# Softmax weights transposed by VectorE and a round trip through HBM, in place of TensorE

## What is computed

```
def _memory_attention(q, mem, w_kv):            # every layer, 4 heads of 64
    ...
    probs = softmax(einsum('bshd,bmhd->bhsm', q, km))
    return einsum('bhsm,bmhd->bshd', probs, vm)
...
w = probs[:, 0] - lam * probs[:, 1]             # layers 0 and 3, 6 heads of 128
return einsum('bhqk,bkhe->bqhe', w, v)
```

## Time and profile before

| | |
|---|---|
| median of 3 runs | 1246.14 us (1246.03 to 1246.64) |
| profiled execution, its span | 1244.7 us |
| TensorE busy | 1235.2 us, 99% of the span |
| VectorE, ScalarE busy | 1024.4 us (82%), 730.3 us (59%) |
| HBM read and written | 226.93 MB, 1.06 MB |

### The profile page before, as it was taken

How to read it: one execution, slowest core, us unless ns; L and a number is a source line. 1 busy time by engine, 2 the same in 40 slices (tenths; PEclk the granted TensorE clock), 3 DMA queues, 4 the chain that set the end, 5 groups by cost and what they waited for, 6 DMA issues and landing times.

```text
span 1244.7 us, 19689 instructions
## 1 busy us (share of the span) xinstructions
PE 1235.2 (99%) x7370; PEld 1082.9 (87%) x7370; DVE 1024.4 (82%) x1599; ACT 730.3 (59%) x1190; POOL 20.1 (2%) x29
## 2 busy tenths in 40 slices
PE   9999999999999999999999999999999999999997
PEld 7988888888999988888889888888888888888886
DVE  5876888889779888988887978988888776988887
ACT  6675765555766546555555546655554774755552
POOL 0001000000000100000000000000000001000000
PEclk9999999999999999999999999999999999999999
DMA  9834576554553345655655764656554533666651
GB/s 333 285 120 136 190 248 190 186 192 163 175 182 119 122 150 169 227 187 195 201 173 168 233 204 162 227 195 199 190 186 169 187 119 119 218 207 201 196 190 54
DMA packets 64539, 229.27 MB, mean 184 GB/s; under 512 B 7575, under 2 KB 9239, under 8 KB 63421
## 3 DMA queue, kind: packets, MB, share of 16 engines
q1 hardware_dynamic: 64444, 228.02, 55.5%
HBM read 226.93 MB, written 1.06 MB: 183 GB/s over the span
## 4 chain that ended last, share of the span: by engine, by line
PE 97%; DMA 1%; SPq 1%; DVE 0%; issue 0%; ACT 0%; DVEq 0%
PE pair L768 28%; PE acc L862 21%; PE pair L771 14%; PE pair L800 4%; PE pair L801 4%; PE pair L802 4%; PE acc L768 2%; PE acc L843 2%; PE acc L842 2%; PE acc L841 2%; PE pair L1022 2%; DMA raw<-in_stream 1%; PE pair L825 1%; PE pair L827 1%; PE pair L829 1%; PE acc L931 1%
## 5 line engine op out<-in xcount | busy, mean ns | idle before, releaser
L1278 DVE TENSOR_TENSOR w_lo<-raw,w_hi 128x1024 fp32r<-128x1024 f32 x400 | 482.6, 1221 | 105.3 <-ACT w_hi L1040 103.7
L1040 ACT ACTIVATE w_hi<-raw 128x1024 fp32r<-128x1024 f32 x400 | 420.5, 1058 | 213.2 <-PE pair L771 70.8
L768 PE MATMUL pair<-xT,w_hi 128*128 128x512 f32 x1520 | 477.8, 396 | 0.0
L771 PEld LDWEIGHTS pair<-xT,w_lo 128*128 128x128 f32 x1520 | 285.5, 188 | 67.2
L771 PE MATMUL pair<-xT,w_lo 128*128 128x256 f32 x1520 | 298.6, 278 | 0.0
L768 PEld LDWEIGHTS pair<-xT,w_hi 128*128 128x128 f32 x1520 | 233.8, 189 | 3.2 <-issue 0.3
L1087 ACT ACTIVATE hid<-pair 128x512 f32<-128x512 f32 x88 | 52.6, 597 | 124.9 <-PE pair L771 124.9
L1319 DVE TENSOR_TENSOR hid<-pair,hid 128x512 f32<-128x512 f32 x88 | 60.7, 690 | 47.9 <-ACT hid L1087 47.7
L800 PE MATMUL pair<-xT,w_hi 128*128 128x256 f32 x336 | 97.8, 291 | 0.0
L801 PE MATMUL pair<-xT,w_hi 128*128 128x256 f32 x336 | 95.0, 283 | 0.0
L802 PE MATMUL pair<-xT,w_lo 128*128 128x256 f32 x336 | 94.9, 283 | 0.0
(11 more groups left out here) (223 smaller groups left out, 1661.9 us busy)
## 6 DMA issues: line engine op xcount, KB each, us to landing
raw<-in_stream SPq DMA_DIRECT2D x400, 512.0 KB, 4.6
gains<-in_ln SPq DMA_DIRECT2D x8, 1024.0 KB, 8.4
bias<-bias_scratch SPq DMA_DIRECT2D x2, 1152.0 KB, 9.0
raw<-in_stream SPq DMA_DIRECT2D x8, 256.0 KB, 6.6
x_tok<-in_x_t SPq DMA_DIRECT2D x4, 256.0 KB, 6.2
y_tok<-in_mem_t SPq DMA_DIRECT2D x2, 512.0 KB, 7.1
x_tok<-in_x SPq DMA_DIRECT2D x1, 1024.0 KB, 6.5
out<-x_tok SPq DMA_DIRECT2D x4, 256.0 KB, 2.0
```

Source lines behind the costliest of these rows:

```text
L768: pe.matmul(bank, w_hi[:, slot, kk * P:(kk + 1) * P], xT[:, kk].rearrange("p a s -> p (a s)"), start=(kk == 0), stop=(kk == KT - 1), skip_ ...
L771: last = pe.matmul(bank[:, 0:SEQ], w_lo[:, slot, kk * P:(kk + 1) * P], xT[:, kk, 0, :], start=False, stop=(kk == KT - 1), skip_group_check ...
L1040: nc.scalar.activation(w_hi[:, u % SPLIT, :], raw[:, u % RAW, :], ACT.Copy).then_inc(hi_ready, 1)
L1278: v.tensor_tensor(w_lo[:, u % SPLIT, :], raw[:, u % RAW, :], w_hi[:, u % SPLIT, :].bitcast(F32), ALU.subtract).then_inc(lo_ready, 1)
```

## The change

TensorE's transposes and ScalarE's copies of them go. In their place:
- xswap and swap: VectorE transposes `prob` in 32x32 blocks within each group of 32 partitions, into `ex` (a pair) or the other half of the `prob` slot (a head). SP stores the result to a scratch tensor in HBM with four DMAs, one for each 32 partitions: 512 KB a pair, 256 KB a head, in runs of 1024 and 512 bytes.
- xfetch and fetch: SP waits until the four stores have landed and reads the scratch back with one DMA, in which the blocks change partitions, to `prob` slot 0 (first pair), `xprobT` (second pair) or `probT`.
- SP, which had a loop over units, now walks through the list of items too.
- xpv and pv wait for the landing. xpv's moving operand comes in runs of 32 floats. `probT` holds four values of one query next to each other, for its four blocks, so pv's stationary operand is read in steps of four floats, 16 bytes.
- In layer 1 the division by the row sum of the cross-attention moves from VectorE to ScalarE.
- In layers 0 and 3 pv(4) and pv(5) go from behind half 19 to behind half 20, and scale(2) from behind half 21 to behind half 22.

```diff
-            at = {0: [it("xlog", 0), it("xlog", 1)], 1: [it("xexp", 0)], 2: [it("xexp", 1), it("xprob", 0)],
-                  3: [it("xprob", 1)], 5: [it("log", 0), it("log", 1)],
-                  6: [it("exp", 0), it("xturn", 0)], 7: [it("exp", 1), it("xpv", 0)],
-                  8: [it("prob", 0), it("xturn", 1)], 9: [it("prob", 1), it("xpv", 1), it("log", 2), it("log", 3), it("turnw", 0)],
-                  10: [it("exp", 2)], 11: [it("turnw", 1), it("exp", 3), it("prob", 2)],
-                  12: [it("prob", 3)], 13: [it("turnw", 2), it("log", 4), it("log", 5), it("pv", 0), it("pv", 1)],
-                  14: [it("ms", 0), it("exp", 4)], 15: [it("turnw", 3), it("tok", 0), it("exp", 5), it("prob", 4)],
-                  16: [it("scale", 0), it("prob", 5)], 18: [it("turnw", 4), it("pv", 2), it("pv", 3), it("turnw", 5)],
-                  19: [it("pv", 4), it("pv", 5), it("ms", 1), it("tok", 1), it("ms", 2)], 20: [it("scale", 1), it("tok", 2)],
-                  21: [it("scale", 2)]}
+            at = {0: [it("xlog", 0), it("xlog", 1)], 1: [it("xexp", 0)], 2: [it("xexp", 1), it("xprob", 0), it("xswap", 0)],
+                  3: [it("xprob", 1), it("xswap", 1), it("xfetch", 0)], 4: [it("xfetch", 1)],
+                  5: [it("log", 0), it("log", 1)], 6: [it("exp", 0)], 7: [it("exp", 1), it("xpv", 0)],
+                  8: [it("prob", 0), it("swap", 0)],
+                  9: [it("prob", 1), it("swap", 1), it("xpv", 1), it("log", 2), it("log", 3), it("fetch", 0)],
+                  10: [it("exp", 2), it("fetch", 1)], 11: [it("exp", 3), it("prob", 2), it("swap", 2)],
+                  12: [it("prob", 3), it("swap", 3), it("fetch", 2)],
+                  13: [it("log", 4), it("log", 5), it("pv", 0), it("pv", 1), it("fetch", 3)],
+                  14: [it("ms", 0), it("exp", 4)], 15: [it("tok", 0), it("exp", 5), it("prob", 4), it("swap", 4)],
+                  16: [it("scale", 0), it("prob", 5), it("swap", 5), it("fetch", 4)], 17: [it("fetch", 5)],
+                  18: [it("pv", 2), it("pv", 3)], 19: [it("ms", 1), it("tok", 1)],
+                  20: [it("scale", 1), it("pv", 4), it("pv", 5)], 21: [it("ms", 2), it("tok", 2)],
+                  22: [it("scale", 2)]}
             at[14].append(("seed", 2 * layer, 0))
             at[16].append(("seed", 2 * layer, 1))
...
-            at = {0: [it("xlog", 0), it("xexp", 0), it("xlog", 1), it("xexp", 1)], 1: [it("xprob", 0), it("xprob", 1)],
-                  4: [it("xturn", 0)], 5: [it("xpv", 0)], 8: [it("xturn", 1)], 9: [it("xpv", 1)]}
+            at = {0: [it("xlog", 0), it("xexp", 0), it("xlog", 1), it("xexp", 1)],
+                  1: [it("xprob", 0), it("xswap", 0), it("xprob", 1), it("xswap", 1)],
+                  2: [it("xfetch", 0)], 3: [it("xfetch", 1)], 5: [it("xpv", 0)], 9: [it("xpv", 1)]}
...
             at = {0: [it("xlog", 0), it("xexp", 0), it("xlog", 1), it("xexp", 1)], 1: [it("xprob", 0), it("xprob", 1)],
-                  4: [it("xturn", 0)], 5: [it("xpv", 0)], 6: [it("xturn", 1)], 7: [it("xpv", 1)]}
+                  2: [it("xswap", 0), it("xswap", 1)], 3: [it("xfetch", 0), it("xfetch", 1)],
+                  5: [it("xpv", 0)], 7: [it("xpv", 1)]}
             at[26], at[28] = [("seed", 2 * layer, 0)], [("seed", 2 * layer, 1)]
...
-            probT = here("probT", [P, HEADS, 2, SEQ])
+            probT = here("probT", [P, HEADS, P, 4])
...
+        def swap_source(n):
+            s = n % 2
+            return (ex[:, s] if items[prob_pos[n]][0] == "xprob" else prob[:, s, 1:2]).rearrange("p i t s -> p (i t s)")
+        def swap_target(n):
+            name, layer, h = items[prob_pos[n]]
+            if name == "prob":
+                return probT[:, h].rearrange("p (a j) c -> p a (j c)", a=4)
+            return (xprobT[:] if h else prob[:, 0].rearrange("p i t s -> p (i t s)")).rearrange("p (a e) -> p a e", a=4)
...
+            for item in items:
+                name = item[0]
+                if name == "begin" and item[1] % 2:
+                    next_unit(item[1] // 2 * 2 + item[2] + RAW)
+                elif name == "lo":
+                    next_unit(item[1] + RAW)
+                elif name in ("xswap", "swap"):
+                    n = weights_of(item)
+                    sp.wait_ge(swapped, n + 1)
+                    for a in range(4):
+                        rows = slice(32 * a, 32 * a + 32)
+                        sp.dma_start(swap_scratch[n][a].rearrange("b i e -> i b e"), swap_source(n)[rows].rearrange(
+                            "i (b e) -> i b e", b=4)).then_inc(swap_stored[n % 2], 16)
+                elif name in ("xfetch", "fetch"):
+                    n = weights_of(item)
+                    if n >= 2:
+                        sp.wait_ge(swap_landed[n % 2], 16 * (n // 2))
+                    if name == "xfetch" and item[2] and item[1]:
+                        sp.wait_ge(xpv_done, 2 * item[1])
+                    sp.wait_ge(swap_stored[n % 2], 64 * (n // 2 + 1))
+                    sp.dma_start(swap_target(n), swap_scratch[n].rearrange("a b i e -> (b i) a e")).then_inc(swap_landed[n % 2], 16)
...
                 elif name == "xpv":
                     layer, pr = item[1:]
                     u = ordinal[pos]
-                    pe.wait_ge(xprobT_ready, 2 * u + 2)
+                    n = weights_of(item)
+                    pe.wait_ge(swap_landed[n % 2], 16 * (n // 2 + 1))
                     pe.wait_ge(vm_ready, layer + 1)
                     bank = side(pos)
+                    weights = swap_target(n).rearrange("p a (i t k j) -> p i k t a j", i=2, t=2, k=2)
                     for k in range(2):
                         for i in range(2):
-                            last = pe.matmul(bank[64 * i:64 * i + 64, 0:SEQ],
+                            last = pe.matmul(bank[64 * i:64 * i + 64, 0:SEQ].rearrange("p (t a j) -> p t a j", t=2, a=4),
                                              vm[:, k, (2 * pr + i) * XHD:(2 * pr + i + 1) * XHD],
-                                             xprobT[:, i, k, :], start=(k == 0), stop=(k == 1))
+                                             weights[:, i, k], start=(k == 0), stop=(k == 1))
                     last.then_inc(xpv_done, 1)
...
                 elif name == "pv":
                     layer, h = item[1:]
-                    u = ordinal[pos]
-                    pe.wait_ge(probT_ready, u + 1)
+                    n = weights_of(item)
+                    pe.wait_ge(swap_landed[n % 2], 16 * (n // 2 + 1))
                     pe.wait_ge(v_ready, values_of(layer, h // 2))
                     bank = side(pos) if h % 2 == 0 else side_bank(pv_pos[layer, h // 2])
                     for t in range(TT):
                         at = ((h % 2) * TT + t) * P
                         for k in range(2):
-                            last = pe.matmul(bank[:, at:at + P], probT[:, h, k, t * P:(t + 1) * P],
+                            last = pe.matmul(bank[:, at:at + P], probT[:, h, :, 2 * t + k],
                                              v_tok[:, k, h * P:(h + 1) * P], start=(k == 0), stop=(k == 1))
...
                     if n >= 2 and logit_name[n - 2] == "xlog":
-                        act.wait_ge(xprob_ready, logit_name[:n - 1].count("xlog"))
+                        act.wait_ge(swap_stored[n % 2], 64 * (n // 2))
...
+                elif name == "xprob" and layer_kind(item[1]) == "hgrn":
+                    n = weights_of(("xswap",) + item[1:])
+                    act.wait_ge(inv_ready, item[2] + 1)
                     for i in range(2):
+                        for t in range(TT):
+                            j = 2 * i + t
+                            last = nc.scalar.activation(prob[:, n % 2, i, t, :], ex[:, n % 2, i, t, :], ACT.Copy,
+                                                        scale=row_inv[:, n % 2, j:j + 1])
...
-                        q = prob_pos[n - 2]
-                        if items[q][0] == "xturn":
-                            dve.wait_ge(xprob_turned, 2 * ordinal[q] + 2)
-                        else:
-                            dve.wait_ge(prob_turned, ordinal[q] + 1)
+                        before, layer, h = items[prob_pos[n - 2]]
+                        if before == "prob":
+                            dve.wait_ge(swap_stored[s], 64 * (n // 2))
+                        elif h == 0:
+                            dve.wait_ge(xpv_done, 2 * layer + 1)
+                    if name == "xprob" and layer_kind(item[1]) == "hgrn":
+                        v.reciprocal(row_inv[:, s, :], row_sum[:, s, :]).then_inc(inv_ready, 1)
...
-                        last.then_inc(prob_ready, 1)
+                        link(last)
+                elif name in ("xswap", "swap"):
+                    n = weights_of(item)
+                    of = prob[:, n % 2] if name == "xswap" else prob[:, n % 2, 0:1]
+                    if name == "xswap" and layer_kind(item[1]) == "hgrn":
```

(19 more changed lines are left out.)

71 lines of the change are left out of this document (18 added, 53 removed).

## The result

The changed kernel takes 1279.76 us (median of 4 runs, 1277.07 to 1282.89) against 1246.2: ratio 1.0271, 95% interval 1.0255 to 1.0287. It is slower by 33.6 us, where the prediction had 7.7 and its range ended at 1265. The sign was right, the size wrong by a factor of more than four.

The account below looks back on a forecast made before the run. TensorE, busy 99% of the span and 97% of the chain, was taken to bound the kernel. Removed transposes -12.2, idle +14.6 and the strided operand +5.3 gave +7.7 us on 1246.1: 1254 us, range 1244 to 1265.

Parts of the forecast that it names:

- the idle time at xpv: TensorE's wait at xpv for the HBM round trip: 0.9, 5.0, 6.8 and 0 us in layers 0 to 3.
- the strided stationary operand: pv's 96 passes, stationary operand read 16 bytes apart: 55 ns more each, 5.3 us; ends 0 and 10.8.
- the clock set at 0: TensorE's granted clock after the two long stalls: no fall in the sum, 6 us more as an upper end.
- the end of the attention layers: Layers 0 and 3: pv(4), pv(5) wait for their fetch, 0.5 us each; the later scale(2) costs 0.3 us each.
- The prediction's own signs of being wrong: Wrong if xpv in layer 2 doesn't wait, or if a pass of pv costs 112 or 220 ns.
- Removed, 12.2 us: TensorE's transposes gone from the chain: 8 xturns at 0.87 us and 12 turnws at 0.44, 12.2 us saved.
- the doubled pass (10.8): Upper end for pv's strided stationary read: 96 passes each 112 ns longer, 10.8 us.
- Rival 2: Everything dearer: transposes of 2.4 us, pv's pass doubled, or the clock falling; 1258 to 1266 us, chance 0.18.
- The 0.3 us for layer 0's logits: Layer 0: VectorE's first transpose pushes the qk that the logits need from 44.47 to 45.6, costing 0.3 us.
- VectorE's transposes and ScalarE's scaled copies at no cost: VectorE's 16.4 us of transposes cost nothing by themselves as it runs ahead; eight scaled copies move to ScalarE in layer 1.
- SP waited 1049 us for w_lo: SP's waits for VectorE's w_lo to free a buffer, read as VectorE, ScalarE and SP running ahead with room.
- Rival 3: Fetch there before xpv(0) comes in layers 1 and 2: 1242 us, or 1237 with the stride free; chance 0.1.

Follow-up runs that it names:

- e12: Kernel before, with the way through HBM for layer 1's cross-attention alone, xpv at 9 and 11: 1245.92 us, ratio 1.0002.
- e13: Kernel before, with the way through HBM for cross-attention in layers 0, 1 and 3; heads and layer 2 stay on TensorE: 1244.62 us, ratio 0.9989.
- e1: Changed kernel with probT in order, so pv's stationary operand is read side by side without the 16-byte step: 1267.41 us, ratio 1.0175.
- e3: Kernel before with only pv's stationary operand read from probT in steps of 16 bytes: 1257.38 us, ratio 1.0095.
- e6: Kernel before with pv's stationary read at steps of 4 to 32 bytes by layer and head pair; 118 ns a pass at 8 bytes, 238 at 32.
- e4: Changed kernel with unused matmuls ahead of xpv(0)'s wait, 30 in layer 1 and 36 in layer 2: 1273.7 us, ratio 1.0225.
- e5: Changed kernel with the last places of the attention layers (pv(4), pv(5), scale and others) as in the kernel before: 1275.95 us, ratio 1.024.
- e11: Kernel before with the change's block transposes added on VectorE, their results unused: 1250.88 us, ratio 1.0037.
- e2: Changed kernel with xpv alone moved later in layers 1 and 2: 1269.77 us, ratio 1.0195.
- e9: Changed kernel with softmax steps spread, pv read in 8-byte steps, VectorE dividing in all layers, xpv later and the tail mended: 1253.46 us, ratio 1.0053.

## Why the prediction was wrong

Most of the mechanism was the forecast one: xpv waits for the round trip, longest in layer 2, then in layer 1, and the strided stationary read adds to it. What failed are sizes of its sum, in order of weight: the idle time at xpv, the strided stationary operand, the clock set at 0, and the end of the attention layers. One of the prediction's own signs of being wrong came up: it called itself wrong if a pass of pv cost 220 ns, and the passes cost 226 to 247.

- **Removed, 12.2 us**: right to about a tenth in the changed kernel, where 1235.2 + 11.7 (pv's step) + 5.1 (the slow clock) less the measured 1240.8 leaves 11.2 for the 112. 16 transposes less took 1.2 us off TensorE's busy time in e12 (their chain time is 1.7), 48 took 4.3 in e13 (5.2).
- **The strided stationary operand, taken at 5.3 us: 11.6 to 12.0 measured.** I read the price off a strided moving operand, which costs 55 ns a pass, and named the doubled pass (10.8) as an end. A stationary read at 16 bytes doubles the pass (e1, e3, e6). Rival 2 had it, with a chance of 0.18.
- **Idle at xpv, 12.7 us taken over the four layers (0.9, 5.0, 6.8, 0): 20.0 measured (1.6, 7.5, 9.2, 1.7).** The mechanism held, with layers 2 and 1 ahead of the rest, and VectorE's part was right to 0.3 us: 1.245 us for a large transpose against 1.15. (The small one took 1.121 us against 0.6, but no fetch of a head was waited for.) Off were two sizes of the trip. A store takes SP 0.43 to 0.44 us to issue (medians of the 48 and the 32), not the 0.33 of a weight load, so eight of them took 3.97 us in layer 1 and not 2.6, all ahead of the fetch: it was issued 3.0 us behind the second transpose where I had 1.9, and in layer 2 2.5 us where I had 1.65. And the fetch landed in 6.8 and 5.9 us, where I had used the medians 5.4 and 4.7. That makes the 2.5 us too much in layer 1 and 2.4 in layer 2. Layer 3's wait I had set at nothing although it runs layer 0's order.
- **The clock, 0 in the sum, 6 us as an upper end: 5.7 measured** (e4; 5.1 in the chain). The term that I left out for want of a row was real and near its end.
- **The end of the attention layers, 1.6 us: 5.2 in waits, 3.9 less time in e5.** Here the wait itself was the wrong one. I looked for the fetch to be late. It wasn't; a_out was. With pv(4) and pv(5) behind scale(1), too little stands between pv and scale(2) to cover the 5.8 us until a_out is there. The 0.3 us for layer 0's logits didn't show as a wait.
- **VectorE's transposes and ScalarE's scaled copies at no cost**: not nothing, and hidden by the stalls. Put into the kernel before, the transposes cost 4.6 us (e11), and once the stalls are gone 9.7 us of new waits stand behind them (e2), 7.7 of them without those of the shared banks. That SP waited 1049 us for w_lo, over the whole span, says nothing of VectorE's room in one stretch: in layer 2 of the kernel before it is busy 97% of the time (690 to 710), which I could have read before.
- **The rivals**: rival 2, everything dearer, was what happened, beyond its 1266 because it took its parts as alternatives; all of them came at once. The step 6.4, the clock 5.7, xpv 7.3 and the end 3.6 more than taken, less the 0.3, are 22.7 us above the sum of 7.7 and make 30.4 of the 30.6 in span. The medians differ by 3 us more: the profiled execution of the changed kernel was the fastest of its runs. Rival 3, the fetch in time, was never near.

What stays open: of e9's 12.2 us of transposes gone, 6.7 show in busy time. Some 1.0 of the 12.2 doesn't show in the changed kernel's busy time either (first point above), a stretch at 0.65 of the clock (704 to 708) takes 1 to 2, pv's steps of 8 bytes 0.6; the other 2 to 3 weren't traced. The changed kernel's executions spread over 5.8 us and those of the kernel before over 0.6; only one of each was traced, so what varies isn't shown. Nor was it tried whether another queue for the fetches shortens the trip.

## What to carry to other kernels

Where one engine is 99% busy and another 82%, "moved to the engine with room" holds only stage by stage: look at the second engine's busy share in the very stretch (here 97% in layer 2, 66% in layer 1), and ask what would be late if the stall you expect were not there to hide it. A stall of 7 us costs its length and then the clock behind it, here 10 us in all. And a layout that interleaves to save a transpose is paid at the operand that is loaded: with float32, 8 bytes were almost free here and 16 doubled the pass.

## What the hardware showed that was not expected

- A stationary load at steps of 4, 8, 12, 16 and 32 bytes makes pv's pass 111, 118, 170, about 235 and 238 ns long: almost free at 8, full price from 16 (e6, one execution; 4 and 16 also in before and e3).
- VectorE's transpose of 128x512 takes 712 ns with its output in runs of 32 elements and 1121 ns with the output at steps of 16 bytes.
- The granted clock fell to 0.50 within the waits of 7.5 and 9.2 us, and stayed at 1.00 through those of 1.6 and 1.7 us in the same execution. It isn't a matter of length alone: in e9 it was 0.65 in the 4 us after a wait of 1.9.

```profile
704.00:708.00 4.00, 3.61 (x13) 3.17 (x14) 3.93 (x6) 0.04 (x1) 0.00 (x0) 0.65 0.96 285
```

- Of 64 KB or 128 KB stores from 32 partitions, SP issues one in 0.43 to 0.44 us (median), against 0.33 for a 512 KB load; whether that is due to the store isn't shown, as the weight loads right behind them took 0.44 and 0.43 too (349.76, 710.33); the trip of one swap from the end of VectorE's transpose to the weights back in SBUF took 9.8 us in layer 1 (347.3 to 357.1), of which the fetch's landing 6.8.
